# A short-convolution and attention block on one core: four chunks of the first projection on un-normalised X

## The reference, cut to what matters

```python
def rmsnorm(x, g):
    y = xf * lax.rsqrt(jnp.mean(xf * xf, axis=-1, keepdims=True) + EPS)
    return (y * g.astype(jnp.float32)).astype(x.dtype)

def modulation(c, w, b, n):
    m = jax.nn.silu(c) @ w + b
    return jnp.split(m, n, axis=-1)

def modulated_norm(x, g, shift, scale):
    return rmsnorm(x, g) * (1.0 + scale[:, None, :]) + shift[:, None, :]

def short_conv_layer(x, c, mod_w, mod_b, norm_g, w_in, conv_w, w_out):
    shift, scale, gate = modulation(c, mod_w, mod_b, 3)
    h = modulated_norm(x, norm_g, shift, scale)
    proj = h @ w_in
    b_gate, c_gate, u, z = jnp.split(proj, 4, axis=-1)
    y = b_gate * causal_dwconv(c_gate * u, conv_w)
    y = y * jax.nn.silu(z)
    return x + gate[:, None, :] * (y @ w_out)
```

## Time and profile before

| what | value |
|---|---|
| median of three runs | 2802.17 us (2800.43 to 2805.7) |
| profiled execution: span from the first to the last instruction, its own time | 2802.3 us |
| PE busy | 2707.3 us, 97% |
| DVE busy | 1614.1 us, 58% |
| ACT busy | 1189.8 us, 42% |
| POOL busy | 1109.0 us, 40% |
| mean granted clock of PE | 0.992 |

### The profile page before, as it was taken

One profiled execution on the slowest core, in us unless ns is written; L12 is line 12 of the kernel. 1 busy time (PEld: TensorE's weight loads), 2 busy tenths in 40 slices (PEclk: granted clock), 3 DMA queues, 4 the chain that ended last, 5 costly groups with the idle time before them and its releaser, 6 DMA issues.

```text
span 2802.3 us, 38646 instructions
## 1 busy us (share of the span) xinstructions
PE 2707.3 (97%) x13208; PEld 2150.3 (77%) x13208; DVE 1614.1 (58%) x2120; ACT 1189.8 (42%) x1779; POOL 1109.0 (40%) x753
## 2 busy tenths in 40 slices
PE   6999999999999998999999999999999999989998
PEld 4788888787777776878886777777788888868886
DVE  7744443304676776583015555554436766788888
ACT  4211123323555555442236667765434433334442
POOL 1222222121555554212221111211123988858886
PEclk9999999999999999999999999999999999999999
DMA  5333321344211213113330101101443343374442
GB/s 228 128 127 120 120 98 45 103 146 140 76 54 45 82 52 114 59 38 111 121 108 31 38 32 37 38 30 61 150 158 120 128 161 141 136 259 158 159 161 92
DMA packets 102110, 294.74 MB, mean 105 GB/s; under 512 B 9856, under 2 KB 10496, under 8 KB 101504
## 3 DMA queue, kind: packets, MB, share of 16 engines
q1 hardware_dynamic: 102016, 293.56, 29.7%
HBM read 220.12 MB, written 73.40 MB: 105 GB/s over the span
## 4 chain that ended last, share of the span: by engine, by line
PE 60%; issue 25%; POOL 6%; DVE 4%; ACT 3%; DMA 1%; POOLq 0%; SPq 0%; ACTq 0%; DVEq 0%
PE PS L847 27%; PE PS L1331 10%; PE PS L1383 5%; PE PS L1077 5%; POOL WL L2747 3%; PE PS L1049 2%; PE PS L982 2%; PE PS L1011 2%; PE PS L1026 2%; PE PS L1235 2%; POOL dL L2860 1%; PE PS L1216 1%; DVE dM L2679 1%; DVE bC L2296 1%; PE PS L1175 1%
## 5 line engine op out<-in xcount | busy, mean ns | idle before, releaser
L2747 POOL TENSOR_TENSOR WL<-WR,WH 128x1024 fp32r<-128x1024 f32 x147 | 367.7, 2501 | 1359.9 <-ACT WH L1421 1252.6
L847 PE MATMUL PS<-HH,WH 128*128 128x512 f32 x1712 | 546.0, 400 | 19.4 <-POOL WL L2747 5.9
L847 PE MATMUL PS<-HL,WH 128*128 128x512 f32 x1712 | 531.6, 392 | 0.0
L847 PE MATMUL PS<-HH,WL 128*128 128x512 f32 x1712 | 530.0, 391 | 0.0
L847 PEld LDWEIGHTS PS<-HH,WH 128*128 128x128 f32 x1712 | 315.4, 189 | 95.9 <-issue 26.3
L847 PEld LDWEIGHTS PS<-HL,WH 128*128 128x128 f32 x1712 | 323.4, 189 | 69.3
L847 PEld LDWEIGHTS PS<-HH,WL 128*128 128x128 f32 x1712 | 323.2, 189 | 69.3
L1421 ACT ACTIVATE WH<-WR 128x1024 fp32r<-128x1024 f32 x147 | 155.6, 1059 | 324.1 <-PE PS L847 226.6
L2771 POOL TENSOR_TENSOR bB<-bB,bC 128x256 f32<-128x256 f32 (+7 forms) x128 | 191.2, 1504 | 191.1 <-DVE bC L2296 191.1
L2296 DVE TENSOR_TENSOR_SCAN bC<-bN,EPSC 128x256 f32<-128x256 f32 (+7 forms) x128 | 222.7, 1751 | 57.3 <-ACT bN L1607 52.4
L2679 DVE TENSOR_TENSOR dM<-PS,dM 128x512 f32<-128x512 f32 x212 | 136.2, 678 | 1.6 <-PE PS L1383 1.2
(11 more groups left out here) (348 smaller groups left out, 5618.7 us busy)
## 6 DMA issues: line engine op xcount, KB each, us to landing
WR<-wst SPq DMA_DIRECT2D x149, 512.0 KB, 3.4
uRAW<-wst SPq DMA_DIRECT2D x32, 512.0 KB, 4.8
hid<-uT SPq DMA_DIRECT2D x32, 512.0 KB, 2.8
dRAW<-wst SPq DMA_DIRECT2D x64, 256.0 KB, 3.6
HLF<-hid SPq DMA_DIRECT2D x28, 512.0 KB, 8.9
GLF<-hid SPq DMA_DIRECT2D x28, 512.0 KB, 8.1
TMP<-mods SPq DMA_DIRECT2D x24, 512.0 KB, 4.2
MR<-mods SPq DMA_DIRECT2D x24, 512.0 KB, 5.3
```

What stands on the lines that cost most here:

```text
L847: last = pe.matmul(PS[:, dst0 + q:dst0 + q + HALF], l, rr[:, k * S + q:k * S + q + HALF], start=a, stop=z)
L2747: pool.tensor_tensor(WL[slot][:, :], WR0[:, :], WH[slot][:, :].bitcast(F32), ALU.subtract).then_inc(w_lo, 1)
```

## The change

- SP loads X in eight blocks, each followed by the scale rows of the same channels; chunks 0 and 1 come between them, chunk 2 and chunk 3 early as well. The shift rows are loaded afterwards into the same places.
- DVE makes only the scale for each k in the first turn; the shift is made in eight further modulations after raw_low(7).
- The squares lie in four buffers in turn, and POOL adds them (seven additions of 128x1024 into XSUM). PE sums over channels once, before step 7, into PAIR[3].
- Chunks 2 and 3 also run on the un-normalised operand, with their own split weights (WHX, WLX) and into PAIR[2] and PAIR[3] (early_step). Their results are read out into AE[2] and AE[3].
- The shift columns of all four chunks are made at once after step 1 of chunk 3 (shift_columns), from the split rows SHR (high and low part side by side), 64 matmuls of two columns.
- Chunks 4 and 5 now take the place of chunks 2 and 3 as the first on the normalised operand. The products of j = 0 are made after the fill.

The diff, cut to its core:

```diff
@@ SyncE
-            for g in range(4):
-                sp.dma_start(X[:, 2 * g * S:2 * (g + 1) * S], xt[:, 2 * g * S:2 * (g + 1) * S]).then_inc(ld_x[g], 16)
...
             for k in range(KT):
-                for m in (k, KT + k):
-                    sp.dma_start(MRAW[:, m * D:(m + 1) * D], mods[m]).then_inc(ld_k[k], 16)
-            load_w(2)
+                sp.dma_start(kt(X, k), xt[:, k * S:(k + 1) * S]).then_inc(ld_k[k], 16)
+                sp.dma_start(kt(MRAW, k), mods[KT + k]).then_inc(ld_k[k], 16)
+                if k == 0:
+                    sp.dma_start(WR0[:, :], wst[0]).then_inc(ld_w, 16)
+                if k == 1:
+                    sp.dma_start(WR1[:, :], wst[1]).then_inc(ld_w1, 16)
+                if k == 5:
+                    sp.wait_ge(ld_w, 16)
+                    sp.wait_ge(w_lo, 1)
+                    sp.dma_start(WR0[:, :], wst[2]).then_inc(ld_w, 16)
+            sp.dma_start(WR3[:, :], wst[3]).then_inc(ld_w3, 16)
+            for k in range(KT):
+                sp.wait_ge(mod_done, k + 1)
+                sp.wait_ge(ld_k[k], 32)
+                sp.dma_start(kt(MRAW, k), mods[k]).then_inc(ld_k[k], 16)
...
             sp.wait_ge(ld_w, 32)
...
             sp.wait_ge(w_lo, 3)
             sp.dma_start(WR0[:, :], wst[4]).then_inc(ld_w, 16)
+            load_w(5)
             sp.wait_ge(f_lo, FILL["a"] + KT)
+            sp.wait_ge(free[1], USED["ain"][1] + 2)
@@ TensorE
+            for k in range(KT):
+                if k == KT - 1:
+                    sum_squares(SQ["aout"], XSUM, dst=3 * S)
+                pe.wait_ge(a_raw_lo, k + 1)
+                step(C_AIN, 0, 0, HH, HL, k)
+                step(C_AIN + 1, 1, 1, HH, HL, k)
+            for k in range(KT):
+                early_step(0, k, None)
+            pe.wait_ge(rs, 1)
+            for k in range(KT):
+                early_step(1, k, a_raw_read)
+                if k == 1:
+                    shift_columns()
...
-                    two_chunks(C_AIN + 2, (0, 1), (0, 1), (u[0] + 1, u[1] + 1), (f_lo, FILL["a"]))
+                    two_chunks(4 * j, (0, 1), (0, 1), (2 * j + u[0], 2 * j + u[1]), (f_lo, FILL["a"]))
@@ ScalarE
+                if k == 2:
+                    split_w(4, 0)
+                    act.activation(SM[:, 12:16], PS[:, S + 1:S + 8:2], ACT.Identity).then_inc(a_shift, 1)
+                if k == 4:
+                    split_w(5, 1)
+                    act.wait_ge(a_shift, 2)
+                    act.activation(AE[1][:, :], AE[1][:, :], ACT.Identity, bias=SM[:, 9:10]).then_inc(ain_cu, 1)
@@ VectorE
+            for k in range(KT):
+                dve.wait_ge(ld_k[k], 48)
+                modulation(col(MOD, k), kt(MRAW, k))
...
+            def early_out(m, pair):
+
+                dve.wait_ge(chunk_done, C_AIN + m + 2)
+                dve.tensor_tensor(AE[m][:, :], PAIR[pair], T[0], ALU.mult).then_inc(free[m % 2], 1)
...
             def first_input(k):
+                if k == 1:
+                    early_out(2, 2)
...
+                if k == 6:
+                    dve.wait_ge(w_lo, 4)
+                    early_out(3, 3)
@@ GpSimd
+            for n in range(KT - 1):
+                pool.wait_ge(sq, n + 1)
+                if n:
+                    pool.wait_ge(sq_added, n)
+                first = XSQ[0] if n == 0 else XSUM
+                pool.tensor_tensor(XSUM[:, :], first[:, :], XSQ[(n + 1) % 4][:, :], ALU.add).then_inc(sq_added, 1)
```

More of the change, by code:

```diff
@@ L416, in block_kernel @@
         ld_cb = sem("ld_cb")
-        ld_x = [sem(f"ld_x{i}") for i in range(4)]
+        ld_vec = sem("ld_vec")
+        ld_w3 = sem("ld_w3")
         ld_k = [sem(f"ld_k{i}") for i in range(KT)]
@@ L421, in block_kernel @@
         ld_w1 = sem("ld_w1")
-        sq_pair = sem("sq_pair")
         ld_w = sem("ld_w")
@@ L903, in _, with early_step @@
             pe.wait_ge(s_const, 1)
[L905 to L910, removed]
-            u = USED["ain"]
+            u = USED["ain"]
+            def early_step(m, k, last_sem):
+                pair = 2 + m
+                b = slice(k * P, (k + 1) * P)
+                if k == 0:
+                    pe.wait_ge(w_hi, C_AIN + 3 + m)
+                    pe.wait_ge(w_lo, C_AIN + 3 + m)
+                last = mm3(pair * S, WHX[m][:, b], WLX[m][:, b], HH, HL, k, k == 0, k == KT - 1)
+                if k == KT - 1:
+                    last.then_inc(chunk_done, 1)
+                elif last_sem is not None:
+                    last.then_inc(last_sem, 1)
@@ new lines, in shift_columns @@
+            def shift_columns():
+                pe.wait_ge(a_rows, 2)
+                pe.wait_ge(free[1], u[1] + 1)
+                for m, (hi, lo) in enumerate(((WH[0], WL[0]), (WH[1], WL[1]), (WHX[0], WLX[0]), (WHX[1], WLX[1]))):
+                    for k in range(KT):
+                        for half in (hi, lo):
+                            last = pe.matmul(PS[:, S + 2 * m:S + 2 * m + 2], half[:, k * P:(k + 1) * P],
+                                             SHR[:, 2 * k:2 * k + 2], start=k == 0 and half is hi,
+                                             stop=k == KT - 1 and half is lo)
+                last.then_inc(a_cols, 1)
@@ L914, in input_chunks @@
             def input_chunks(j, first=False):
                 if first:
[L916 to L927, removed]
@@ L928, in input_chunks @@
-                    two_chunks(C_AIN + 2, (0, 1), (0, 1), (u[0] + 1, u[1] + 1), (f_lo, FILL["a"]))
-                for n in range(4 if first else 0, 4):
+                    two_chunks(4 * j, (0, 1), (0, 1), (2 * j + u[0], 2 * j + u[1]), (f_lo, FILL["a"]))
+                for n in range(2 if first else 0, 4):
                     chunk(4 * j + n, n % 2, n % 2, 2 * j + (u[n % 2] + n // 2))
-            input_chunks(0, first=True)
-            with pe.Fori(1, KT) as j:
+            input_chunks(1, first=True)
@@ L934, in _ @@
+            with pe.Fori(2, KT) as j:
                 input_chunks(j)
```

176 lines of the change are left out of this document (95 added, 81 removed).

## The result

The changed kernel takes 2825.5 us (median of 4 runs, 2820.6 to 2827.8) against 2801.3 us of the kernel before in the same session: ratio 1.0082, interval 1.0068 to 1.0097, so 19 to 27 us slower. The forecast was 2809.0 us, with a range that ended at 2815. The profiled spans are 2823.2 and 2802.3 us.

The account below looks back on a forecast made before the run. PE, busy 97% of the span, was taken as the bound, with chunk 7's wait deciding. The product 5.7 us later plus 1 us for the clock gave 2802.3 + 6.7 = 2809.0 us; own range 2804.5 to 2813.5, whole range 2800 to 2815.

Parts of the forecast that it names:

- What bounds the start: First stage: chunk 7's wait for the product that frees PSUM pair 1 decides, not how much earlier chunk 0 starts.
- The exclusion: In the start, DVE instructions with two on-chip inputs stand while POOL runs, so 20.7 and 21.1 us add up.
- First leg: To the end of chunks 0 and 1: 53.6 us, 7.2 us earlier than before.
- Second leg: From the end of chunks 0 and 1 to step 2 of chunk 3: 14.9 + 6.3 us, ending at 74.8 us.
- Third leg: From step 2 of chunk 3 to the product for chunk 7: a longer chain across engines, ending at 128.8 us.
- The start in all: The product for chunk 7 comes 5.7 us later than before, plus 1 us for the clock: +6.7 us.
- Behind it the order is as in before, where PE never waits again, so nothing is given back.: After the product for chunk 7: nothing further changes, so the start's +6.7 us reaches the span unchanged.
- The rivals: No exclusion in the start 8%, 2792 us; tail covered 12%, 2797; half clock 10%, 2817; losses and gains cancel 5%, 2802.
- Half clock through the start: Rival, 10%: clock stays at 0.5, turns of 5.1 us, chunks 0 and 1 end 8 us later, 2817 us.

Follow-up runs that it names:

- the late modulations: Six modulations of j = 0 put behind the first product of j = 1, loads reordered: changed kernel with SHR behind GL 2802.4 us; kernel before 2800.8 us.
- The four edits: Changed kernel with SHR behind GL, additions of squares on DVE, shift columns in four groups, modulations of j = 0 behind the product: together 2790.4 us, ratio 0.9968.

## Why the prediction was wrong

- **What bounds the start: right.** The product on pair 1 ended chunk 7's wait, and when it was freed of the modulations the time fell by 6 us.
- **The exclusion: right.** COEF at 2.21 us beside every addition, a turn of 4.6 us (4.9 forecast: COEF's own 0.22 us lie inside the wait for POOL, and the addition starts 0.16 us before it). The Trainium skill, "SBUF — State Buffer", section "Who interferes with whom", agrees; the reading of "Advanced Engine Details and Errata", section "VectorE Performance Modes", that only the 2-port modes contend does not: a float32 operation with two tensors stood still here.
- **First leg: right.** Chunks 0 and 1 end at 53.2 us, 53.6 forecast.
- **Second leg: the shift columns were mis-sized.** The term was 64 products at the price of the row of 8 in 0.79 us, 6.3 us. They took 10.5 us, since the clock fell to half while they ran, and the step behind them ran at half clock as well (2.7 in place of 1.36 us). I had bounded the price by the half-clock row, 14.7 us, but did not ask what a block of 64 small products does to the clock; spread over four steps they ran at 1.00 throughout. Of the consequence I had the direction, not the size: 1.2 us less were forecast with the columns at their low bound of 3.2 us, and 4 us less were measured without them.
- **Third leg: right within 2 us.** From the end of step 2 of chunk 3 to the end of the product I had 54.0 us; it took 52.2 us (80.4 to 132.6). The small steps of its sum add to 9.85 us where it says 10.0, and PE's own arrival to 121.1 us where it says 121.6; neither changes the forecast. With the second leg 5.6 us late and the third 1.8 us short the product ended 3.8 us later than forecast.
- **The start in all.** +6.7 us were forecast. With SHR behind GL, the changed kernel costs 8.7 us (5.9 to 11.8), so this part of the sum lies within its error.
- **The step that failed: "Behind it the order is as in before, where PE never waits again, so nothing is given back."** The order was the same. "Never waits again" holds for the stretch to 200 us that I had read; over the rest PE waits 57.1 us in before, and 54.5 us in the changed kernel, so waits did not grow. But the time of one product did. From start to start, in before and in the changed kernel: 864 products of GH and GL with WH and WL, 0.2268 and 0.2332 us (5.6 us in all); 672 of GH and GL with the weights of the feed-forward's first half, 0.2287 and 0.2320 (2.2 us), and 672 with those of its second half, 0.2271 and 0.2330 (3.9 us); 216 whose operand lies over the moved tiles, 0.2267 and 0.2330 (1.4 us). With 0.2 us for HH and HL in the feed-forward that is some 13 us. Measured are 23.0 − 8.7 = 14.3 us by the ratios of the two runs of the changed kernel, and 14.0 us (9 to 19) by the unused tile in the kernel before. One line of the diff did it, `SHR = place("SHR", 2 * KT, F32R)`, and I read it as storage only.
- **The rivals.** None of the four held this, and 2825.5 us lies above all of them. "Half clock through the start" had 2817 us; the clock was 0.80 to 1.00 up to 55 us, so it was not that either.

The late parts of two single profiles differ by a few us more than this, since the stretches of half clock fall differently in each execution (the kernel before ranged from 2793 to 2806 us); I have used ratios of medians for sizes and the profiles for places. Left open: why the chip is slower when weights and moving operand lie 128 bytes apart, and whether moving the additions to DVE gains the 3.9 us that its profile shows at 400 us or the 0.3 us between the ratios.

## What to carry to other kernels

A line that places a tile is a change to every tile behind it: look at where operands of the long products lie against each other (here modulo 256 bytes), put new small tiles last, and compare the time of the same instruction in a stretch that the change doesn't touch before explaining anything by order. A gain at the head of a chain counts only as far as the next fixed link lets it through: here the late modulations gave 6 us in the changed kernel and nothing in the kernel before, where the wait was short and the next one stood right behind. The four edits on the changed kernel are worth less than 1 up to 14 us one by one, 26 in sum, and gave 32 us together; that they do more together than in sum is not shown, as the two figures differ by less than their error. Small products in one long block can cost clock on top of their own time: at 0.112 us each the 64 would have taken 7.2 us, they took 10.5, and the step behind them 1.3 us more than at full clock. Between full-sized ones the same 64 kept the clock.

## What the runs showed of the hardware

- A product of 128x512 in fp32r starts every 0.2267 us when weights and moving operand lie alike modulo 256 bytes (384 products with GH and GL in the kernel before), and every 0.2333 us when they lie 128 bytes apart (the same 384 in the changed kernel); for HH and HL with WH and WL 0.2267 and 0.2324 us. Moving both by 128 (0.2267 us, ratio 0.9990), or one by 256 (0.2267 us, ratio 1.0003), changes nothing. Products that lie alike but follow a group of six that lie apart take some 0.003 us more than others.
- 64 two-column products, each with new weights, went at 0.112 us from start to start at a granted clock of 1.00 and at 0.213 us at half clock; in one block of 64 the granted clock fell (0.52 from 70 to 80 us), in four groups of 16 between full products it stayed at 1.00.
- DVE's product of one column with two on-chip inputs stood 2.2 us beside POOL's addition of two float32 tensors, and took 0.22 us alone; POOL's addition takes 2.36 us where DVE's takes 1.22.
